# A hybrid attention layer on one Trainium2 core: half of the branch product moved into the steps of the second attention half

## What is computed

```python
proj = h @ w_in
...
a = jnp.where(visible, jnp.exp(jax.nn.log_sigmoid(z) + excl), 0.0)      # SB: o_sb = a @ v
...
p = jax.nn.softmax(logits, axis=-1)                                     # DS: o_ds = p @ v
...
gates = jax.nn.sigmoid(jnp.concatenate([g_sb, g_ds], axis=-1) + b_gate)
gate_sb, gate_ds = gates[..., :D_MODEL], gates[..., D_MODEL:]
merged = gate_sb * (o_sb @ w_branch_sb) + gate_ds * (o_ds @ w_branch_dsa)
return merged @ w_out
```

## Time and profile before

| | |
|---|---|
| median of 3 runs | 1745.53 us (1737.97 to 1750.38) |
| the profiled execution | 1746.8 us, span 1745.0 us |
| TensorE busy | 1638.4 us (94%) |
| VectorE busy | 1245.4 us (71%) |
| ScalarE, POOL busy | 851.5 us (49%), 539.7 us (31%) |
| mean granted TensorE clock | 0.972 |

### The profile page before, as it was taken

The page is one execution under the profiler, slowest core; times in us unless marked ns, Lnnn a source line. Parts: engine busy times, 40 slices in busy tenths (PEclk is TensorE's granted clock), DMA queues, the critical chain, the costliest instruction groups (busy, mean ns, idle before and its releaser), DMA issues. The chain is left out here.

```text
span 1745.0 us, 23454 instructions
## 1 busy us (share of the span) xinstructions
PE 1638.4 (94%) x8360; PEld 1384.4 (79%) x8360; DVE 1245.4 (71%) x1966; ACT 851.5 (49%) x1650; POOL 539.7 (31%) x332
## 2 busy tenths in 40 slices
PE   4999899999999999889889999989999999999997
PEld 4889888799877777777777878768888878888885
DVE  5287798888988989687873435785454548777878
ACT  5266555555445545576751133555555543333334
POOL 1111254555434435321102450475545510000000
PEclk6999999999999999998989999999999999999999
DMA  4564434344233233355304443243444365443434
GB/s 172 155 194 124 128 120 134 108 137 114 89 106 107 92 106 107 91 134 135 86 1 163 139 169 121 72 158 133 145 149 174 136 229 217 157 159 131 169 138 103
DMA packets 101372, 231.23 MB, mean 133 GB/s; under 512 B 11192, under 2 KB 25848, under 8 KB 101256
## 3 DMA queue, kind: packets, MB, share of 16 engines
q1 hardware_dynamic: 100680, 227.64, 40.7%
q0 software_dynamic: 576, 2.10, 0.7%
HBM read 155.83 MB, written 73.86 MB: 132 GB/s over the span
## 5 line engine op out<-in xcount | busy, mean ns | idle before, releaser
L710 PE MATMUL bk<-x_hi,w_hi 128*128 128x512 f32 (+2 forms) x832 | 308.7, 371 | 1.2 <-PEq L353 1.2
L710 PE MATMUL bk<-x_lo,w_hi 128*128 128x512 f32 (+2 forms) x832 | 299.3, 360 | 0.0
L710 PE MATMUL bk<-x_hi,w_lo 128*128 128x512 f32 (+2 forms) x832 | 298.5, 359 | 0.0
L666 POOL TENSOR_TENSOR pt_lo<-a_buf,pt_hi 128x512 fp32r<-128x512 f32 (+3 forms) x104 | 138.4, 1347 | 193.0 <-ACT pt_hi L930 192.8
L334 POOL TENSOR_TENSOR w_lo<-w_raw,w_hi 128x1024 fp32r<-128x1024 f32 x53 | 130.4, 2460 | 190.9 <-ACT w_hi L330 190.7
L1087 DVE TENSOR_SCALAR_CACHE_REDUCE counted<-sc,small 128x272 uint8<-128x272 f32 (+6 forms) x217 | 182.5, 891 | 0.9
L1674 PE MATMUL bank<-v_hi,f_hi 128*128 128x512 f32 x448 | 174.3, 389 | 0.0
L1674 PE MATMUL bank<-v_hi,f_lo 128*128 128x512 f32 x448 | 174.3, 389 | 0.0
L1674 PE MATMUL bank<-v_lo,f_hi 128*128 128x512 f32 x448 | 174.3, 389 | 0.0
L710 PEld LDWEIGHTS bk<-x_hi,w_lo 128*128 128x128 f32 x832 | 158.5, 191 | 17.6
L710 PEld LDWEIGHTS bk<-x_hi,w_hi 128*128 128x128 f32 x832 | 159.1, 191 | 16.1 <-issue 1.3
(11 more groups left out here) (228 smaller groups left out, 3861.0 us busy)
## 6 DMA issues: line engine op xcount, KB each, us to landing
w_raw<-w_units SPq DMA_DIRECT2D x57, 512.0 KB, 3.7
f_raw<-f_d SPq DMA_DIRECT2D x28, 1024.0 KB, 5.0
u_raw<-w_units SPq DMA_DIRECT2D x32, 512.0 KB, 4.8
f_d<-f_s SPq DMA_DIRECT2D x64, 256.0 KB, 2.2
b<-w_units SPq DMA_DIRECT2D x16, 1024.0 KB, 8.3
f_d<-c SPq DMA_DIRECT2D x48, 256.0 KB, 2.1
k_hi<-k_d SPq DMA_DIRECT2D x32, 260.0 KB, 5.6
k_lo<-k_d SPq DMA_DIRECT2D x32, 260.0 KB, 6.1
```

The costliest lines, as they stand in the source:

```text
L666: pool.tensor_tensor(pt_of(pt_lo, j, tiles), raw, pt_of(pt_hi, j, tiles).bitcast(F32), ALU.subtract).then_inc(sb_lo, 1)
L710: mm = pe.matmul(pj[b][:, 0:c1 - c0], w[:, s, kt, :], a[:, kt, c0:c1], start=kt == 0 and k == 0, stop=kt == KT - 1 and k == 2)
```

## The change

- The first two `o_raw` reads keep their place or nearly so, and the four are now four steps apart: `RELOAD` = 70, 74, 78, 82.
- From step 66 on TensorE runs the products of part 0 behind `turn`, `values` and `turn_sums`. The ring of banks for transposes loses bank 0 and is 4, 5, 6 to the end.
- The SB half of the branch product is cut in 16 parts (k, and half of the columns), each of four triples of matmuls into bank 0 (`branch_part`). The 64 triples are dealt over the 76 places (two per step) of steps 88 to 125, one place behind `turn` and one before the products of part 1. VectorE multiplies a finished part by its gate (`gate_part`), at the end of its own step; SP stores it to DRAM (`m1_d`) and loads the gate for the part after next, behind a head's loads if these fall in the step. A part's first triple waits for the multiplication of the part before.
- The units of the branch matrices are regrouped: units 43 to 46 hold the SB matrix, 47 to 50 the DS one, and one unit now serves two k. Four units are loaded, rounded and split within the steps.
- The branch stage is left with 24 matmuls per k (DS). It loads the DS gate and the stored product; VectorE multiplies, adds (no longer POOL) and makes `m_lo` one k later.

```diff
-RELOAD = [NJ // 2 + 6 + 10 * p_ for p_ in range(4)]
+RELOAD = [NJ // 2 + 6 + 4 * p_ for p_ in range(4)]
...
-    ring = (4, 5, 6) if j < NJ // 2 + 2 else (4, 5, 6, 0)
     TPN[key] = len(TP_BANK)
-    TP_BANK.append(min(ring, key=lambda b: max([n for n, x in enumerate(TP_BANK) if x == b], default=-1)))
+    TP_BANK.append(min((4, 5, 6), key=lambda b: max([n for n, x in enumerate(TP_BANK) if x == b], default=-1)))
...
+PARTS = 2 * KT
+B_STEPS = [(j_, part_) for j_ in range(RELOAD[3] + 6, NJ - 2) for part_ in range(2)]
+B_FILL = [[[], []] for _ in range(NJ + 6)]
+for n_ in range(4 * PARTS):
+    j_, part_ = B_STEPS[n_ * len(B_STEPS) // (4 * PARTS)]
+    B_FILL[j_][part_].append(divmod(n_, 4))
...
+                def store_part(m):
+                    u, k, c = part_at(m)
+                    sp.wait_ge(part_gated, m + 1)
+                    sp.dma_start(m1_d[k * P:(k + 1) * P, c * HALF:(c + 1) * HALF], m1_st[:, m % 2]).then_inc(m1_out[m % 2], 16)
+                    if m + 2 < PARTS:
+                        load_gate(m + 2)
...
+                def branch_part(m, h):
+                    u, k, c = part_at(m)
+                    if h == 0:
+                        if m == 0:
+                            pe.wait_ge(or_lo, 4)
+                            bank_read(NC_ALL - 2 + NC_ALL % 2)
+                        else:
+                            pe.wait_ge(part_gated, m)
+                        pe.wait_ge(lo_done, u + 1)
+                    for n, (w, a) in enumerate(((w_hi, o_hi), (w_hi, o_lo), (w_lo, o_hi))):
+                        mm = pe.matmul(bk[0][:], w[:, u % 2, 4 * (k % 2) + h, :], a[:, h, c * HALF:(c + 1) * HALF], start=h == 0 and n == 0,
+                                       stop=h == 3 and n == 2)
+                    if h == 3:
+                        mm.then_inc(part_mm, 1)
...
-                    for k, slots in PRODUCTS[j][0]:
-                        product(k, slots)
+                    if j < SECOND_HALF:
+                        for k, slots in PRODUCTS[j][0]:
+                            product(k, slots)
...
+                    for m, h in B_FILL[j][0]:
+                        branch_part(m, h)
+                    if j >= SECOND_HALF:
+                        for k, slots in PRODUCTS[j][0]:
+                            product(k, slots)
+                    for m, h in B_FILL[j][1]:
+                        branch_part(m, h)
...
+                def gate_part(m):
+                    dve.wait_ge(gate_sb_in[m % 2], 16 * (m // 2 + 1))
+                    if m >= 2:
+                        dve.wait_ge(m1_out[m % 2], 16 * (m // 2))
+                    dve.wait_ge(part_mm, m + 1)
+                    dve.tensor_tensor(m1_st[:, m % 2], bk[0][:], gate_sb[:, m % 2], ALU.mult).then_inc(part_gated, 1)
...
-                    dve.tensor_tensor(gated[:, k % 2, 0], bank[2 * (k % 2)][:], gate[:, k % 2, 0], ALU.mult)
-                    dve.tensor_tensor(gated[:, k % 2, 1], bank[2 * (k % 2) + 1][:], gate[:, k % 2, 1], ALU.mult).then_inc(br_free, 1)
...
+                        dve.tensor_tensor(gated[:, k % 2, 0], bank[2 + k % 2][:], gate[:, k % 2, 1], ALU.mult).then_inc(br_free, 1)
+                        dve.wait_ge(br_free, k + 1)
+                        dve.tensor_tensor(gated[:, k % 2, 0], gated[:, k % 2, 0], gate[:, k % 2, 0], ALU.add).then_inc(add_done, 1)
```

More of the change, by code:

```diff
@@ L497, in build @@
             ki_in, wt_t, wt_done = sem("f_kiin"), sem("f_wtt"), sem("f_wtok")
-            qi_in = [sem(f"f_qiin{h}") for h in range(HI)]
+            landed = [sem(f"landed{h}") for h in range(HI)]
+            qi_in = landed
             s_ready, s_relu, s_acc, search_op = (sem("f_" + n) for n in ("sready", "srelu", "sacc", "search"))
@@ L625, in _ @@
                         load_unit(sp, u + 2, u % 2)
+                    for m in B_STARTS[j]:
+                        if m % 4 == 0:
+                            u = part_at(m)[0]
+                            load_unit(sp, u + 2, u % 2)
                     for part in range(2):
@@ L637, in _ @@
                         load_head(g)
+                    for m in B_ENDS[j - 1][0] + B_ENDS[j - 1][1] if j else []:
+                        store_part(m)
+                    if j == RELOAD[3] + 4:
+                        sp.wait_ge(or_lo, 4)
+                        load_gate(0)
+                        load_gate(1)
                     for p in range(4):
@@ L981, in _ @@
                         evacuate(n)
+                    for m in B_ENDS[j][0]:
+                        next_unit(m)
                     if 2 <= j < NJ + 2:
@@ L989, in _ @@
                         evacuate(n)
+                    for m in B_ENDS[j][1]:
+                        next_unit(m)
                     for p in range(4):
@@ L1182, in scale_pair @@
                         else:
+                            dve.wait_ge(m1_out[half], 16 * KT)
                             dve.tensor_copy(r_last[:, cols], src).then_inc(tp_free, 1)
@@ L1249, in _ @@
                             rest(n)
+                        for m in B_ENDS[j][0] + B_ENDS[j][1]:
+                            gate_part(m)
                     due += SEARCH[j][1]
@@ L1332, in build @@
             t_rounded, t_rest, t4_raw = (sem("t_" + n) for n in ("trnd", "trest", "t4raw"))
-            u_in = [sem(f"m_u{r}") for r in range(RING)]
+            u_in, QI_LANDED = landed[:RING], 64
             w_sum, s_hi_done, s_lo_done, product, copied, added = (sem("m_" + n) for n in ("wsum", "shi", "slo", "prod", "copy", "add"))
@@ L1374, in _ @@
             def _(sp):
+                for i in range(2):
+                    sp.wait_ge(m1_out[i], 16 * KT)
                 for k in range(KT):
                     if k >= 2:
[L1377 to L1380 removed]
+                        sp.wait_ge(add_done, k - 1)
+                    sp.dma_start(gate[:, k % 2, 1], g_d[D + k * P:D + (k + 1) * P, :]).then_inc(g_in5[k % 2], 16)
+                    sp.dma_start(gate[:, k % 2, 0], m1_d[k * P:(k + 1) * P, :]).then_inc(g_in5[k % 2], 16)
+                    if k % 2 == 0:
+                        u = U_BRANCH_DS + k // 2
+                        load_unit(sp, u + 2, u % 2)
                 for v in range(V0, V0 + 6):
                     load_ring(sp, v)
[L1383 removed]
+                sp.wait_ge(add_done, KT)
                 sp.dma_start(rr[:, 0], x[0:P, :]).then_inc(x_in[0], 16)
@@ L1567, in _ @@
                         pe.wait_ge(br_free, k - 1)
-                    for t in range(2):
-                        outs = [(bank[2 * (k % 2) + t][:, c * HALF:(c + 1) * HALF], c * HALF, (c + 1) * HALF) for c in range(2)]
-                        mm = unit_mm(pe, u % 2, o_hi, o_lo, outs, kts=range(4 * t, 4 * t + 4),
-                                     before=lambda kt: pe.wait_ge(last_out, 2) if k == 0 and kt == KT - 1 else None)
+                    outs = [(bank[2 + k % 2][:, c * HALF:(c + 1) * HALF], c * HALF, (c + 1) * HALF) for c in range(2)]
+                    mm = unit_mm(pe, u % 2, o_hi, o_lo, outs, kts=range(at0, at0 + 4), a_of=lambda kt: 4 + kt % 4,
+                                 before=lambda kt: pe.wait_ge(last_out, 2) if k == 0 and kt == 3 else None)
                     mm.then_inc(br_done, 1)
@@ L2217 @@
     units += [unit(w_in, 3368 + P * j) for j in range(2 * KT)]
-    branches = np.concatenate([f(w_branch_sb)[0], f(w_branch_dsa)[0]], axis=0)
-    units += [unit(branches, P * j) for j in range(KT)]
+    for branch in (f(w_branch_sb)[0], f(w_branch_dsa)[0]):
+        units += [unit(np.concatenate([branch[:, 2 * P * j:2 * P * j + P], branch[:, 2 * P * j + P:2 * P * j + 2 * P]], axis=0), 0) for j in range(4)]
     units += [f(w_out)[0][P * j:P * j + P] for j in range(KT)]
```

69 lines of the change are left out of this document (42 added, 27 removed).

## The result

The changed kernel takes 1785.3 us (median of 4 runs, 1784.3 to 1785.9) against 1742.0 us of the kernel before beside it: ratio 1.0248, 95% interval 1.0207 to 1.0288. It is 43 us slower. I had forecast 1741 us and a range of 1718 to 1762; the time lies outside, on the slow side. The forecast started from the profiled execution of 1746.8 us, 5 us over that median; as a change it was -5.5 us, and +43 is what came.

A forecast was written before the change was run, and what follows sets the result against it. Matmuls bound the branch stage, a chain from scores over VectorE and ScalarE the loop, and TensorE steps 88 to 127 after the change. -43.5 + 33 + 5 = -5.5 against 1746.8 us gave 1741 us, range 1718 to 1762.

The forecast's parts named there:

- Branch stage, -43.5: Branch stage: 192 of 384 matmuls go, 0.227 us each, with VectorE and DMAs charged nothing: 43.5 us saved.
- The rival that it would not shrink: Branch stage: VectorE or DMA set its pace, so it gets no shorter: 1755 us or more, chance 0.05.
- Steps 70 to 88, +5: Loop steps 70 to 88: three reload rounds take 39 us against 33; +5 us in all, ends 0 and +9.
- the earlier transposes give a little back, the smaller ring takes it: Steps 70 to 88: the reorder's small gain and the smaller ring's cost cancel; no size of their own.
- (b): Steps 88 to 127: TensorE waits for a bank filled in the same step at the values' second half, 4 us.
- (d): Steps 88 to 127: the sums need two more banks just filled, 1.4 us each, 3 us.
- The triples, +33: Steps 88 to 127: 134.5 us of TensorE work plus 12 us of waits make 146.5 us for 113.2, +33.
- Only some 21 us of the 48.5 can hide: Steps 88 to 127: of 48.5 us of added TensorE work, some 21 us fit without lengthening the stretch.
- the first rival: Loop steps absorb most of the added work: stretch grows by 13 us, 1717 us in all, chance 0.27.
- TensorE is the bound of these steps: Steps 88 to 127: TensorE's 134.5 us of work exceed the old 113.2, so TensorE sets their length.
- The single bank: Steps 88 to 127: TensorE waits 7 to 8 us at part changes; as a rival 33 us, 1769 us, chance 0.15.
- The clock: Heads 11 to 15: granted clock near full; only a rival charged a slow-clock stretch, at 3 us.

The follow-up runs named there:

- four buffers: Product behind the transposes, ring of three, late reload rounds, four instead of two weight buffers for pairs 32 to 55: 1760.1 us, against 1788.8 us with two.
- the version without a closed chain: Changed kernel with the first product ahead of the transposes again and the parts taking banks by turns from the ring of four: 1741.3 us, ratio 0.9994.

## Why the prediction was wrong, step by step

- **Branch stage, -43.5:** right (-44.1 between the stretches), and VectorE and the DMAs kept up at 248 GB/s. The rival that it would not shrink falls.
- **Steps 70 to 88, +5:** 14 measured. The reload rounds are 5 or 6 of it; the failed step is the sentence behind them, "the earlier transposes give a little back, the smaller ring takes it". It priced the reorder as a small gain and the ring as no more than that gain; the ring's other terms, (b) and (d), 7 us in steps 88 to 127, were priced one by one. Measured, order and ring cost 5 and 12 us alone and 41 together, of which four buffers gave back 29, so what was missing is the chain product, rounding, rest, bank, next transposes. I had read what the product waits for and not who waits for the product: ScalarE's `pv_done`, in `round_weights`, was in the code, and the profile had 43 us of ScalarE's idle time ahead of that rounding, put down to the transposes.
- **The triples, +33:** in the version without a closed chain the term is -1.0 + 44.1 - 6.3 = 37 us. That version has neither (b) nor (d); without them (7 of the 17 us that I took as 12) my term would be about 28, so the size was too small by some 9 us even there. In the change it is 10 + 44 = 54, because triples stand ahead of the product (13 us) and on one bank (waits of 16 us, 6 of which come back when the parts are dealt apart).
- **"Only some 21 us of the 48.5 can hide":** a misreading of its own sum. 134.5 less 113.2 is what can't hide; 27 us could. The forecast of +33 used the sum and stands, but the first rival was given too little room. In the version with the parts in the ring, four heads hid 3 us.
- **"TensorE is the bound of these steps":** right only for the version with parts in the ring. In the change TensorE is busy 83%, less than before the change (87%).
- **The single bank:** forecast 7 to 8 us, waits of 16 us. The Trainium skill's rule on rotating banks (Perfetto Trace Analysis, Matmuls) gave 28 us by my count, so the 16 lie between the two. Dealing the parts apart gave back 6 us; the 15 us between the version with the product ahead and the one with parts in the ring hold the ring's share too.
- **The clock:** I expected it near full, and charged a slow stretch only in one rival. It was 0.92 in steps 88 to 127, and 0.82 in steps 64 to 87 (0.90 before).
- **The range:** its upper end came from the single bank alone. No case had the reorder as a loss.
- **ScalarE idle 2 us ahead of the reload copies:** not seen in the kernel after, whose steps are longer. With the reload rounds alone it is there, in three waits of 3.9 us together.

## What to carry to other kernels

Before moving a matmul group behind another, list who waits for it, and first the waits that free a buffer: with two buffers, the consumer's end is the producer's start. Two edits that each take slack from the same chain of waits must be priced together: here they cost 5 and 12 us alone and 41 together. And look at the granted clock beside the waits, since in the kernel after a wait of 2.15 us had some 10 us at 1.2 GHz behind it.

## What the runs showed of the hardware

The same 928 matmuls took 136 to 159 us of busy time in six kernels, at granted clocks of 0.97 to 0.85 and with 22.0 to 35.8 us of idle time between them. In the kernel after, the clock fell to 1.2 GHz within a wait of 2.15 us and stayed there for some 10 us.
